# A two-layer hybrid decoder trunk on one core: norms and projections at the sublayer boundaries, handled by halves of the tokens

## What is computed

```python
def rms_norm(x, g):
    return x * lax.rsqrt(jnp.mean(x * x, axis=-1, keepdims=True) + EPS) * g

def swiglu_ffn(h, w_in, w_out):              # w_in 1024 x 5632, w_out 2816 x 1024
    a, b = jnp.split(h @ w_in, 2, axis=-1)
    return (jax.nn.silu(a) * b) @ w_out

def modulated_sublayer(x, fn, g_pre, g_post, m, res_w):
    shift, scale, gate = m[:, 0], m[:, 1], m[:, 2]
    h = rms_norm(x, g_pre) * (1.0 + scale) + shift
    return x + res_w * gate * rms_norm(fn(h), g_post)

for l in range(2):
    mod = (silu(c) @ w_ada[l] + b_ada[l]).reshape(bsz, 3, 3, 1024)
    x = modulated_sublayer(x, ffn1, ..., 0.5)
    x = modulated_sublayer(x, token_mixing, ..., 1.0)   # HGRN2, stick-breaking and dilated
    x = modulated_sublayer(x, ffn2, ..., 0.5)           # attention, gated, merged, projected
```

## Time and profile before

| | us |
|---|---|
| median of 3 runs | 3137.53 (3135.73 to 3139.64) |
| profiled execution | 3135.97, its span 3134.0 |
| TensorE busy | 2901.4 (93%), 13775 records |
| VectorE busy | 1612.5 (51%) |
| ScalarE busy | 987.4 (32%) |
| GpSimd busy | 315.6 (10%) |
| mean granted TensorE clock | 0.962 of full speed |
| transfers | 336.69 MB, 107 GB/s |

### The profile page before, as it was taken

The page is one execution under the profiler, slowest core; times in us unless marked ns, Lnnn a source line. Parts: engine busy times, 40 slices in busy tenths (PEclk is TensorE's granted clock), DMA queues, the critical chain, the costliest instruction groups (busy, mean ns, idle before and its releaser), DMA issues. The chain is left out here.

```text
span 3134.0 us, 34269 instructions
## 1 busy us (share of the span) xinstructions
PE 2901.4 (93%) x13775; PEld 2355.2 (75%) x13775; DVE 1612.5 (51%) x2147; ACT 987.4 (32%) x1374; POOL 315.6 (10%) x264
## 2 busy tenths in 40 slices
PE   5999987989999988999969999789899999799996
PEld 4888766877888766888758878577788887588885
DVE  6555237776255446542265542577743554555324
ACT  3322124444322333222232221344442232322212
POOL 2000003221100012000020000222210002200001
PEclk7999998999999998999989999899999999899998
DMA  7555322222122234542235542222212131355321
GB/s 250 168 186 184 109 81 71 65 61 68 28 68 82 94 108 134 186 124 95 81 95 187 188 163 94 74 68 64 59 54 53 55 108 68 107 188 175 94 94 67
DMA packets 368749, 336.69 MB, mean 107 GB/s; under 512 B 13005, under 2 KB 310353, under 8 KB 367697
## 3 DMA queue, kind: packets, MB, share of 16 engines
q1 hardware_dynamic: 367056, 332.35, 33.5%
q10 hardware_dynamic: 1536, 2.16, 0.2%
HBM read 326.01 MB, written 6.29 MB: 106 GB/s over the span
## 5 line engine op out<-in xcount | busy, mean ns | idle before, releaser
L700 PE MATMUL PS<-HH,WH 128*128 128x512 f32 x2512 | 1013.8, 404 | 41.4 <-DVE HL L1354 23.0
L702 PE MATMUL PS<-HH,WL 128*128 128x512 f32 x2512 | 986.4, 393 | 0.0
L701 PE MATMUL PS<-HL,WH 128*128 128x512 f32 x2512 | 984.7, 392 | 0.0
L1371 DVE TENSOR_TENSOR WL<-RAW,WH 128x2048 fp32r<-128x2048 f32 x148 | 339.2, 2292 | 532.2 <-ACT WH L1049 432.2
L700 PEld LDWEIGHTS PS<-HH,WH 128*128 128x128 f32 x2512 | 476.0, 189 | 154.2 <-issue 35.6
L702 PEld LDWEIGHTS PS<-HH,WL 128*128 128x128 f32 x2512 | 475.1, 189 | 102.8
L701 PEld LDWEIGHTS PS<-HL,WH 128*128 128x128 f32 x2512 | 476.4, 190 | 95.7 <-issue 3.8
L1107 ACT ACTIVATE WH<-RAW 128x2048 fp32r<-128x2048 f32 x88 | 168.7, 1917 | 395.8 <-PE PS L702 395.8
L700 PE MATMUL PS<-GH,WH 128*128 128x512 f32 x704 | 283.2, 402 | 0.0
L702 PE MATMUL PS<-GH,WL 128*128 128x512 f32 x704 | 279.5, 397 | 0.0
L701 PE MATMUL PS<-GL,WH 128*128 128x512 f32 x704 | 279.5, 397 | 0.0
(11 more groups left out here) (218 smaller groups left out, 3226.3 us busy)
## 6 DMA issues: line engine op xcount, KB each, us to landing
RAW<-in_ffn_w_in SPq DMA_DIRECT2D x180, 512.0 KB, 5.2
AW<-in_w_ada SPq DMA_DIRECT2D x288, 256.0 KB, 4.8
RAW<-in_w_in SPq DMA_DIRECT2D x132, 512.0 KB, 4.8
RAW<-in_ffn_w_out SPq DMA_DIRECT2D x88, 512.0 KB, 4.4
AWB<-in_w_ada SPq DMA_DIRECT2D x5, 2048.0 KB, 16.0
RAW<-in_w_out SPq DMA_DIRECT2D x16, 512.0 KB, 4.0
x_kept<-X SPq DMA_DIRECT2D x2, 2048.0 KB, 7.4
X<-x_kept SPq DMA_DIRECT2D x2, 2048.0 KB, 8.9
```

The source lines that it names most:

```text
L700: pe.matmul(o, ah, bh, start=start, stop=False)
L701: pe.matmul(o, ah, bl, start=False, stop=False)
L702: return pe.matmul(o, al, bh, start=False, stop=stop)
L1371: dve.tensor_tensor(WL[slot][:, 0:n], RAW[slot][:, 0:n], WH[slot][:, 0:n].bitcast(F32), ALU.subtract).then_inc(w_low, 1)
```

## The change

Both layers become one block, with every semaphore's target counted on from layer to layer (`at`), so that the clearing, the second layer's special weight groups and the last block go away. X at the boundaries is worked on by two halves of 256 tokens.

- PSUM holds y by halves: `y_at(half, j)` puts tiles j and j+1 of the first half into banks 0 to 3 and those of the second into banks 4 to 7. All row groups therefore issue products of 256 columns, twice as many. So do the first two groups behind every boundary (`first_pair`), half 0 with all eight tiles, then half 1.
- The last two row groups run together, column by column: tile 7 of both halves, then tiles 0 to 6 of half 0, then tiles 0 to 6 of half 1. Their start waits for both groups' weights.
- The first two groups behind a boundary have weight slots of their own (WXH, WXL), in memory that the third last row group still reads; theirs and the row groups' `w_used` and `y_done` order this (`free`, `beside`).
- Between half 1's products stand the sums of half 0's norms (`pair_sums`, `x_sum`), and between the first pair's products of half 0 those of half 1's second norm. y's squares are added in pairs as before; X's squares are not, so TensorE sums eight of them in each half.
- VectorE makes Z = y * gain * root straight out of PSUM and adds two tiles at once to X (`residual`); GpSimd has no work at the boundaries.
- The first stick-breaking pair is item 1 of the mixers, in PSUM banks 2 and 3, the first value item is item 2; BQ and BK have a third buffer.
- The last layer leaves out the five modulation chunks that nothing reads (`chunks`). Half of the final copies out of PSUM go to ScalarE.

The diff, cut to its core:

```diff
@@ MIX @@
+    if _h == 0:
+        MIX.append(("b", COL_BQ, COL_BK))
@@ semaphores @@
+    def at(sem, n):
+        return now[0] * per_layer[sem.num] + n
@@ weight slots @@
+    def free(g):
+        if beside(g):
+            back = max((e for e in ROW_ENDS if e <= g), default=0) - 3
+        else:
+            back = g - (4 if beside(g - 2) else 2)
+        if back >= 0:
+            return used(back)
...
+    def y_at(half, j):
+        return PS[:, 4 * half + j // 2, HALVES[j % 2]]
@@ TensorE @@
-                def norm_sum(n, q):
-                    pe.wait_ge(n_ss, 4 * n + q + 1)
-                    pe.matmul(PS[:, 1 - n % 2, :], ones, NSS[q][:, :], start=(q == 0), stop=(q == 3)).then_inc(n_mm, 1)
+                def x_sum(p, half, q):
+                    pe.wait_ge(x_sq, at(x_sq, 8 * p + 4 * half + q + 1))
+                    for e in range(2):
+                        mm = pe.matmul(y_at(half, 0), ones, XSQ[q][:, e, :], ...)
...
+                    for half in range(2):            # first_pair
+                        cols = HALVES[half]
+                        order = [(k, u, i) for k in range(KT // 2 if half else KT) for u in range(2) for i in range(2)]
+                        if half:
+                            order += [(k, u, i) for u in range(2) for i in range(2) for k in range(KT // 2, KT)]
+                        for n, (k, u, i) in enumerate(order):
+                            if (u, i) == (0, 0):
+                                input_tile(p, half, k)
+                            mm = three(PS[:, 2 * u + i, cols], ..., HH[:, k, cols], HL[:, k, cols], k == 0, True, True)
+                            if not half and p and (u, i) == (1, 1) and k >= KT // 2:
+                                x_sum(p, 1, k - KT // 2)
...
+                    for i in range(n - 2):           # rows_product
+                        pe.wait_ge(w_low, at(w_low, g0 + i + 1))
+                        ready(i)
+                        for half in (1, 0) if i == 0 else (0, 1):
+                            for j in range(KT):
...
+                                mm = column(i, j, half)
+                        mm.then_inc(w_used, 1)
+                    pe.wait_ge(w_low, at(w_low, g0 + n))
...
+                    column(n - 2, 7, 0)
+                    column(n - 1, 7, 0)
+                    ends(1, 7)
+                    for j in range(KT - 1):
+                        if j == 6:
+                            pe.wait_ge(y_copied, at(y_copied, b + 1))
+                        ends(0, j)
+                    for j in range(KT - 1):
+                        ends(1, j)
+                        if j == 0:
+                            pair_sums(b, 0)
+                        if 3 <= j < 6 and not last:
+                            x_sum(b + 1, 0, j - 3)
+                        if j == 5 and not last:
+                            x_sum(b + 1, 0, 3)
+                    pair_sums(b, 1)
@@ ScalarE @@
+                    for q in range(4):               # boundary, behind root_y(b, 0)
+                        if q == 3 and not last:
+                            root_x(b + 1, 0)
+                        square_y(b, 1, q)
+                        if q in (1, 2) and not last:
+                            square_x(b + 1, 0, 2 * q - 2)
+                            square_x(b + 1, 0, 2 * q - 1)
+                    root_y(b, 1)
@@ VectorE @@
-                            dve.tensor_tensor(X[:, j, :], X[:, j, :], Y[:, j, :], ALU.add).then_inc(x_odd, 1)
+                        dve.scalar_tensor_tensor(Z[q][:, e, :], y, POST[:, s, j:j + 1], NR1[:, cols],
+                                                 ALU.mult, ALU.mult).then_inc(z_done, 1)
...
+                    dve.tensor_tensor(x, x, Z[q][:, :, :], ALU.add).then_inc(x_done, 1)
+                    inputs(b + 1, 0, lambda q: residual(b, 1, q))
+                    inputs(b + 1, 1)
+                    low(g + 2)
@@ GpSimd @@
-                        pool.tensor_tensor(X[:, j, :], X[:, j, :], Y[:, j, :], ALU.add).then_inc(x_even, 1)
```

More of the change, by code:

```diff
@@ L110 @@
 NTURNS = len(TURN_OF)
-ROW_LASTS = (G_MIX - 1, G_FFN2 - 1, NG - 1)
+ROW_ENDS = (G_MIX, G_FFN2, NG)
+HALVED = tuple(g for e in ROW_ENDS for g in (e - 2, e - 1))
+HALVES = (slice(0, SEQ // 2), slice(SEQ // 2, SEQ))
+Y_ENDS = 9
 def used_count(g):
-    return sum(x not in ROW_LASTS for x in range(g + 1))
+    return sum(x not in HALVED for x in range(g + 1))
 def loads_of(g):
@@ L587, in _ @@
                 dve.tensor_copy(MOD[:, 4 * ch - 4:4 * ch], PS[:, 5 - ch % 2, 0:4]).then_inc(first_out, 1)
-    for l in range(DEPTH):
-        with nc.Block() as block:
+    with nc.Block() as block:
             @block.sync
@@ L1095, in ffn_in, with output @@
+                def output(half):
+                    for n in range(4 * half, 4 * half + 4):
+                        i, j = n // 2, n % 2
+                        if half and j:
+                            continue
+                        act.wait_ge(res_turned, at(res_turned, n + 1))
+                        act.activation(XIN[:, i, j * SEQ:(j + 1) * SEQ], PS[:, n, :], ACT.Copy).then_inc(res_out[0], 1)
                 def ffn_in(f, g0):
@@ new lines, in inputs @@
+                def inputs(p, half, between=None):
+                    for j in range(KT):
+                        input_scaled(p, half, j)
+                        if j:
+                            input_low(p, half, j - 1)
+                        if j % 2 and between:
+                            if j == KT - 1:
+                                input_low(p, half, j)
+                            between(j // 2)
+                    if not between:
+                        input_low(p, half, KT - 1)
@@ new lines, in boundary @@
+                def boundary(b, g):
+                    last = b == 3 * DEPTH - 1
+                    if not last:
+                        low(g)
+                    pair_add(b, 0, 0)
+                    pair_add(b, 0, 1)
+                    if not last:
+                        low(g + 1)
+                    pair_add(b, 0, 2)
+                    pair_add(b, 0, 3)
+                    for q in range(4):
+                        residual(b, 0, q)
+                        if q:
+                            pair_add(b, 1, q - 1)
+                    pair_add(b, 1, 3)
+                    if last:
+                        for q in range(4):
+                            residual(b, 1, q)
+                        return
+                    inputs(b + 1, 0, lambda q: residual(b, 1, q))
+                    inputs(b + 1, 1)
+                    low(g + 2)
```

1093 lines of the change are left out of this document (557 added, 536 removed).

## The result

The changed kernel takes 3119.9 us (median of 5 runs, 3118.73 to 3125.22) against 3137.59 (5 runs of the kernel before): ratio 0.9948, 95% interval 0.9936 to 0.996, so 12.5 to 20 us less. I forecast 3139. The time lies inside my widest range (3106 to 3168) but outside that of the forecast itself (3123 to 3155), and the forecast was wrong: I expected no change, and the change is real. It lies between the forecast and rival A's 3111, and has the size of neither.

The account below looks back on a forecast made before the run. TensorE, busy 93%, was taken as the bound, with pauses at sublayer boundaries. Terms -27.6 + 20 + 24.0 + 2.3 - 7.2 + 1.7 - 4.1 + 1.0 - 8 gave +2.1 us: 3139, own range 3123 to 3155, widest 3106 to 3168.

Parts of the forecast that it names:

- rival A: Clock stays 2.4 GHz except after the first wait, cut GH loses its surcharge, boundary chains 1 us tighter: 3111; chance 0.23.
- The start: Before the first boundary: roots no earlier, first weight group in the loop waits for a recently freed slot; 1.7 us more.
- Row groups outside the walk: Cut products not counted in the boundary estimate: 1,728 GH and 192 HH at 0.0125 us each, 24.0 us more.
- Inner boundaries with the clock and GH's pace: Five inner sublayer boundaries: 27.6 us less, then 20 more for low clock and 2.3 more for GH halves' pace.
- The last boundary: From the last two row groups to the span's end: 49.9 us including clock, 7.2 less.
- The chunks: Last layer without five modulation chunks, whose column sums take some 0.8 us each of TensorE's queue: 4.1 us less.
- The mixers with the clock: First value item waits less for VectorE's copies: 4 us less a layer, 8 in all (0 to 12).
- I take the middle, 0.0125: Extra cost of cutting one GH product, between 0.0065 us (surcharge vanishes) and 0.0185 (it returns with each half).
- The waits of 1.1 and 0.6 us for VectorE's tiles: Inner boundary: VectorE, also carrying the second half's residual, needs 3.5 us for two tiles, TensorE 2.9.
- The clock's term: Low clock after waits at inner boundaries: 4 us each, 20 in all (bounds 1.7, and 10 if it stays low).
- B: Slower rival: first wait lowers the clock until the boundary is over, 5.6 us more a boundary, 28 in all: 3167; chance 0.22.
- Rival C: The 4.5 us wait before the last two row groups does not appear, weights come earlier: 39 less, 3100; chance 0.05.

Follow-up runs that it names:

- the experiment: Changed kernel with the last layer's five modulation chunks kept: 3125.01 us, 5.1 more.
- The kernel with both orders: Changed kernel with nine columns of the second last row group before the wait for the last group's weights, and ScalarE's X squares before y's: 3083.74 us.
- Five changes of order: Changed kernel with early second-last-group columns, X squares before y's, first two tiles biased before y's root, X sums earlier, y sums later: 3051.51 us.

## Why the prediction was wrong

**The sum, term by term**, from the landmarks of both traces. The start: +3.3 against +1.7 (the last two row groups begin 6.1 us later, of which 432 cut products are 2.8). Row groups outside the walk: +24.0 forecast; 1,728 x 0.0065 + 192 x 0.0125 = +13.6 by what was measured, which is the low bound I had given. Inner boundaries with the clock and GH's pace: -27.6 + 20 + 2.3 = -5.3 forecast, -16.1 measured. The last boundary: -7.2, -8.5. The chunks: -4.1, and the experiment says -5.1. The mixers with the clock: -8 forecast, some -2 measured (from the end of one boundary's work to the start of the next, with the 48 products added as in the prediction, the layers differ by +0.2 and +0.4 us, and w_out's cuts are +1.2 in each). Their sum is -13.8 with the chunks at 4.1, the spans differ by 14.7; the wait for `ada_out`, +1.0, was not seen as a term of its own.

**The step that failed first** is "I take the middle, 0.0125". Both bounds stood there, 0.0065 and 0.0185, each a mechanism, and the middle belonged to neither: it was the HH rows' value laid on another tile. The cut of GH takes its surcharge away, 0.0062 us measured. That is 10.4 us outside the walk, more than the 6.3 us that can be told from none. The earlier trace rows could not decide it: they hold no half with GH. But rows of this case with a slower 512-column product and no word on why are a reason to hold the ends apart, and I gave the cheap end 0.23 as a part of rival A only.

**The second step** is the inner boundary, as large in all as the first: 76.1 us with the clock and 0.5 for GH, against 73.7 in the first one and 73.9 in the mean, 10.8 us over the five. Products 46.1 and sums 10.4 were right. The waits of 1.1 and 0.6 us for VectorE's tiles came to 0.4, for two reasons. VectorE's round for two tiles, from Z to the next Z in the changed kernel, is 3.10 us, and I had costed it at 3.5:

```profile
480.52 0.87 DVE L1494 SCALAR_TENSOR_TENSOR Z<-PS,POST,NR 128x256 f32<-128x256 f32 x2
...
483.62 0.87 DVE L1494 SCALAR_TENSOR_TENSOR Z<-PS,POST,NR 128x256 f32<-128x256 f32 x2
```

And the clock is low just there (481.60 to 485.00), where TensorE needs 0.2135 us a product and is itself the later one. The kernel with both orders has the same 60 products at full clock; its stretch, then the changed kernel's:

```profile
472.88:481.13 8.25, 7.70 (x60) 7.30 (x61) 8.15 (x19) 3.12 (x7) 0.00 (x0) 1.00 0.00 1
```
```profile
480.75:489.69 8.94, 8.91 (x61) 8.62 (x62) 8.84 (x21) 3.81 (x9) 0.00 (x0) 0.81 0.00 1
```

At 0.1195 us a product 60 take 7.17 us, so at full clock the waits are 1.1 us, not 1.7: 0.6 of the miss is VectorE's round. The slow stretch then adds 0.7 us and not the 1.3 to 1.5 of its 14 to 16 slow products: the other 0.7 is a wait and a slow clock that lie beside each other, and that I had added. Together 1.3 us a boundary; the rest is 0.4 of clock (3.6 against 4) and the 0.5 for GH. The clock's term itself was about right, and rivals A (high but for the first wait) and B (low until the end) both fell: two stretches, 6.8 and 3.4 us, or three of 3.4 in the fourth boundary.

**The third** pointed the other way. The mixers' first pause did go (2.05 us idle before, none after), the second stayed at 2.78 idle (2.99 before): the copy that it waits for stands behind 3.9 us of VectorE work, most of it head 0's (518.88 to 522.76). Other pauses grew, one from 0.44 to 1.74 us idle (at 782.6), so that TensorE's idle time over a layer's mixers fell only from 34.3 to 33.5 us. I had named this failure ("a head's chain shows as a pause like the 2.99 us one") and costed it at nothing. Its 6 us offset part of the 21 us of the first two steps, so that the forecast was not further off is luck.

**Rival C** (the wait of 4.5 us absent) fell by the pause at 442.32. Of what would show the forecast right nearly all came: pauses under 5 us, the first of 4.55, 24 sums, boundaries of 73.6 to 74.3 us, clock 0.975. The GH halves, at 0.1185 to 0.120, lie at or under the lower edge of my 0.120 to 0.126, and that edge is the cheap cut of the first step. Most of the pieces were right and the time was not, because three terms that I could have bounded were each taken at one value, and two of them erred on the same side.

**Where the expected gain lies.** The changed kernel still has 13 us of pauses in each inner boundary, and low clock costs it 37 us behind the first 400. Five changes of order take 68 us off it, without one product fewer: 3051.5, against 3119.9 and before's 3138.

## What to carry to other kernels

When a term rests on an operation that no row shows, and its two ends are two mechanisms, keep them as two cases or find the row that tells them apart; the middle is a value no mechanism gives. Where a wait for another engine and a slow stretch fall on the same place, do not add them: here half of the slow stretch's cost was hidden in the wait. And when a chain is cut to run beside products, read each in-order queue for an instruction that waits for the newest product while ready work stands behind it: here ScalarE had two such, and with TensorE's own orders they were worth four times what the change brought.

## What the runs showed of the hardware

- A 512-column product takes 0.2267 us reading HH, 0.232 reading GH with the same values in it, and 0.2335 reading GH with its own; cut in two, its halves take 0.237 to 0.240 together. Cutting costs 0.0131 us with HH and 0.0062 with GH.
- GpSimd's and VectorE's adds of 512 columns beside each other take 1.64 us each, VectorE's alone 0.69. VectorE doing both made this kernel 10.5 us faster. No run shows GpSimd's add alone.
- Less waiting can mean less clock: with the two 1.49 us pauses gone, TensorE worked 96 us at 1.2 GHz instead of 85 (behind 400 us, one trace of each); with the first pause gone too, 57; with all pauses of the first boundary under 1.2 us idle, 30.
